# Layer one of a four-layer network: inverses of chunk matrices on packed 32x32 blocks

## What is computed

```python
def rwkv7_step(state, inp):
    r_t, w_t, k_t, v_t, kk_t, a_t = inp
    sa = jnp.einsum('bhvk,bhk->bhv', state, -kk_t)
    state = (state * w_t[:, :, None, :]
             + sa[..., None] * (kk_t * a_t)[:, :, None, :]
             + v_t[..., None] * k_t[:, :, None, :])
    y = jnp.einsum('bhvk,bhk->bhv', state, r_t)
    return state, y
```

## Time and profile before

| | us |
|---|---|
| median of three timed runs (1768.96 to 1769.55) | 1769.27 |
| the profiled execution | 1763.46 |
| its span, first to last instruction | 1761.7 |
| TensorE busy, share of the span | 1678.9, 95% |
| VectorE busy | 1279.4, 73% |
| ScalarE busy | 804.2, 46% |
| GpSimd busy | 827.7, 47% |
| TensorE weight loads, beside the products | 1287.2, 73% |

### The profile page before, as it was taken

How to read it: one execution, slowest core, us unless ns; L and a number is a source line. 1 busy time by engine, 2 the same in 40 slices (tenths; PEclk the granted TensorE clock), 3 DMA queues, 4 the chain that set the end, 5 groups by cost and what they waited for, 6 DMA issues and landing times.

```text
span 1761.7 us, 34351 instructions
## 1 busy us (share of the span) xinstructions
PE 1678.9 (95%) x13932; PEld 1287.2 (73%) x13932; DVE 1279.4 (73%) x2255; ACT 804.2 (46%) x1489; POOL 827.7 (47%) x727
## 2 busy tenths in 40 slices
PE   5899999999999899989999999999999999999997
PEld 5677777787787667757777777787777778777766
DVE  7599999999999788268998777535887536355553
ACT  3534444444453173365534444434767533444443
POOL 3544354354353245457883222544555545545433
PEclk9999999999999999999999999999999999999998
DMA  7212312312313133212221111133222232433322
GB/s 305 93 65 64 119 52 71 121 50 74 121 51 132 37 91 129 86 60 72 84 85 59 37 37 37 49 96 108 77 80 74 87 102 76 139 121 112 114 57 90
DMA packets 51885, 154.84 MB, mean 88 GB/s; under 512 B 5888, under 2 KB 12032, under 8 KB 51600
## 3 DMA queue, kind: packets, MB, share of 16 engines
q1 hardware_dynamic: 51728, 152.65, 26.7%
HBM read 150.50 MB, written 2.13 MB: 87 GB/s over the span
## 4 chain that ended last, share of the span: by engine, by line
PE 37%; DVE 13%; issue 3%; ACT 3%; POOL 2%; DVEq 0%; POOLq 0%; ACTq 0%
PE bank L524 8%; PE bank L528 8%; PE bank L525 8%; PE bank L2350 3%; DVE best L2458 2%; DVE lru_xc L2842 2%; DVE score L2461 2%; PE bank L3067 1%; PE bank L2380 1%; DVE probs_t L2505 1%; PE bank L3082 1%; POOL w_lo L498 1%; PE bank L570 1%; DVE score L2445 1%; PE bank L571 1%
## 5 line engine op out<-in xcount | busy, mean ns | idle before, releaser
L498 POOL TENSOR_TENSOR w_lo<-raw,w_hi 128x512 fp32r<-128x512 f32 (+2 forms) x434 | 581.3, 1355 | 587.7 <-ACT w_hi L480 573.6
L524 PE MATMUL bank<-h_hi,w_hi 128*128 128x512 f32 x1368 | 573.6, 419 | 10.2 <-ACT h_hi L977 2.2
L528 PE MATMUL bank<-h_lo,w_hi 128*128 128x512 f32 x1368 | 539.2, 394 | 7.6 <-DVE h_lo L945 5.7
L525 PE MATMUL bank<-h_hi,w_lo 128*128 128x512 f32 x1368 | 537.5, 393 | 0.0
L480 ACT ACTIVATE w_hi<-raw 128x512 fp32r<-128x512 f32 (+2 forms) x434 | 247.6, 603 | 247.4 <-PE bank L528 162.1
L524 PEld LDWEIGHTS bank<-h_hi,w_hi 128*128 128x128 f32 x1368 | 258.7, 189 | 99.2 <-issue 39.1
L528 PEld LDWEIGHTS bank<-h_lo,w_hi 128*128 128x128 f32 x1368 | 258.2, 189 | 72.6 <-DVE h_lo L945 10.8
L525 PEld LDWEIGHTS bank<-h_hi,w_lo 128*128 128x128 f32 x1368 | 259.3, 190 | 57.0 <-issue 9.3
L1581 DVE SCALAR_TENSOR_TENSOR ya<-padded,vecs,ya 128x512 f32<-128x512 f32 x240 | 217.4, 906 | 3.9
L3143 DVE CUSTOM_DVE_ANT_0 fox_probs<-bank,fox_keybias 128x128 f32<-128x128 f32 (+3 forms) x64 | 28.9, 489 | 84.6 <-PE bank L3067 84.3
L524 PE MATMUL bank<-own_hi,w_hi 128*128 128x512 f32 x208 | 83.2, 400 | 3.9 <-POOL w_lo L498 3.9
(11 more groups left out here) (410 smaller groups left out, 2865.6 us busy)
## 6 DMA issues: line engine op xcount, KB each, us to landing
raw<-even_in SPq DMA_DIRECT2D x57, 512.0 KB, 3.6
raw<-odd_in SPq DMA_DIRECT2D x39, 512.0 KB, 3.5
raw<-ada SPq DMA_DIRECT2D x32, 512.0 KB, 4.2
raw<-fox_in SPq DMA_DIRECT2D x25, 512.0 KB, 3.5
raw<-lru_in SPq DMA_DIRECT2D x24, 512.0 KB, 3.5
ada_first<-ada SPq DMA_DIRECT2D x16, 512.0 KB, 13.4
raw<-even_out SPq DMA_DIRECT2D x16, 512.0 KB, 3.5
raw<-odd_out SPq DMA_DIRECT2D x16, 512.0 KB, 3.5
```

The source lines that it names most:

```text
L498: e.tensor_tensor(k.w_lo[s % NSPLIT][:, at], k.raw[n % NRAW][:, at], k.w_hi[s % NSPLIT][:, at].bitcast(F32), ALU.subtract).then_inc(*did(" ...
L524: e.matmul(out, hi[:, w], x[i][0], start=start and i == 0, stop=False, skip_group_check=True)
L525: e.matmul(out, lo[:, w], x[i][0], start=False, stop=False, skip_group_check=True)
L528: m = e.matmul(out, hi[:, w], x[i][1], start=False, stop=stop and i == kt - 1, skip_group_check=True)
```

## The change

The inverse is made on 32x32 blocks that are packed side by side. With 32 columns for each of eight matrices and four partition quarters, a buffer [128, 256] holds the 32 diagonal blocks of the 16 matrices, and half of a W buffer is enough. `N` is computed so that the diagonal blocks of both kinds of quarter come to lie in the same columns (48 narrower products for 16), and ScalarE also copies the whole. Helper `quarters` replaces `four`: 32 products of 32x32 on the four diagonal tiles, into 256 columns of one bank. The transposed squares are still second sets of products on TensorE (`sq1_t`, `sq2_t`), copied by VectorE; N transposed, and both turns of the merges, are transposes of VectorE. The first merge stays inside the packed blocks. The last merge gives the one off-diagonal 32x32 block of each matrix, and copies put the packed inverses into PT (ScalarE the upper halves, VectorE the rest). MM holds three blocks of 64 columns a chunk, not four. The start masks change with this.

Apart from that, `out_scalar` and `out_gpsimd` get `begun`, set for even, odd and fox: the weights of the third out block are rounded ahead of the activations. In fox the early roundings, their rests and the first two out blocks get other places in the order.

```diff
@@ -1008,6 +1004,8 @@
 
     def blocks():
         yield 0.0
+        if begun:
+            round_ahead(k, e, need, did, k.nth[(name, *out_order()[0])] + NSPLIT)
...
 
-    def four(name, p, lhsT, rhs, until, *ready):
-        (bank,), free = banks(name, p, 1, until)
+    def quarters(name, p, lhsT, rhs, until, *ready):
+        bank, free = k.work.take(*until)
+        k.bank[name, p, 0] = bank
         wait(*free, *ready)
         for n in range(2 * TT):
-            h, c = divmod(n, TT)
-            for g, gs in HALVES:
-                m = mul(bank[gs, at_chunk(n)], lhsT[gs, h, c, :], rhs[gs, h, c, :])
+            cols = slice(n * KB, (n + 1) * KB)
+            for qs in QUARTERS:
+                m = mul(bank[qs, cols], lhsT[qs, cols], rhs[qs, cols])
         m.then_inc(*did("multiplied", name, p))
 
...
+                            j, col = 2 * c + g, (c % 2) * 3 * CH + x * 2 * CH
+                            m = mul(bank[h][gs, col:col + (2 - x) * CH].rearrange("p (a t) -> p a t", t=CH), src[hs, j, :],
+                                    AR[hs, x:, j, :])
             m.then_inc(*did("multiplied", ("mm", half), p))
         yield at["N"]
...
+        taken = [k.work.take(("activated", "N", p, h)) for h in range(2)]
...
         for c in range(TT):
             for g, gs in HALVES:
                 for h, hs in HEADS:
...
+                    j = 2 * c + g
+                    out, right = taken[h][0][:, at_chunk(c)], B[hs, j, :]
+                    mul(out[QUARTERS[2 * g], 0:KB], AR[hs, 0, j, 0:KB], right[:, KB:])
+                    mul(out[QUARTERS[2 * g], KB:], AR[hs, 0, j, 0:KB], right[:, 0:KB])
+                    m = mul(out[QUARTERS[2 * g + 1], :], AR[hs, 0, j, KB:], right)
...
         yield at["sq1"]
...
+        quarters("sq1", p, N_t, N, [("activated", "sq1", p)], ("made", "N_t", p))
+        quarters("sq1_t", p, N, N_t, [("made", "sq1", p)])
         yield at["sq2"]
...
+        quarters("sq2", p, N2_t, N2, [("activated", "sq2", p)], ("activated", "sq1", p), ("made", "sq1", p))
+        quarters("sq2_t", p, N2, N2_t, [("made", "sq2", p)])
         yield at["sq2p"]
...
+        quarters("sq2p", p, N2, inner, [("made", "sq2p", p)], ("pooled", "inner", p))
         yield at["sq3"]
...
+        quarters("sq3", p, N4_t, N4, [("activated", "sq3", p)], ("activated", "sq2", p), ("made", "sq2", p))
         yield at["sq3p"]
...
+        quarters("sq3p", p, N4, inner, [("made", "sq3p", p)], ("made", "sq2p", p))
         yield at["sq4"]
...
+        quarters("sq4p", p, N8, inner, [("made", "sq4p", p)], ("activated", "sq3", p), ("made", "sq3p", p))
+        yield at["off0"]
+        quarters("off0", p, below, inner, [("activated", "off0", p)], ("pooled", "below", p), ("made", "sq4p", p))
+        yield at["merge0"]
+        quarters("merge0", p, N_t, N, [("made", "merge0", p)], ("made", "turn0", p), ("activated", "off0", p))
+        yield at["off1"]
+        bank, free = k.work.take(("activated", "off1", p, 0), ("activated", "off1", p, 1))
+        k.bank["off1", p, 0] = bank
+        wait(*free, ("made", "merge0", p), ("activated", "N", p, 1))
+        for n in range(2 * TT):
+            h, c = divmod(n, TT)
+            for g in range(2):
+                m = mul(bank[QUARTERS[2 * g], n * KB:(n + 1) * KB], k.NN[QUARTERS[2 * g + 1], h, c, 0:KB],
+                        inner[QUARTERS[2 * g + 1], n * KB:(n + 1) * KB])
+        m.then_inc(*did("multiplied", "off1", p))
+        yield at["merge1"]
+        bank, free = k.work.take(("made", "merge1", p))
+        k.bank["merge1", p, 0] = bank
+        wait(*free, ("made", "turn1", p), ("activated", "off1", p, 0), ("activated", "off1", p, 1))
+        for n in range(2 * TT):
+            cols = slice(n * KB, (n + 1) * KB)
+            for q, qs in enumerate(QUARTERS):
...
+def solve_buffers(k):
+
+    N, N_t, N2, N2_t, N4, N4_t, N8, below = (w[:, s, :, :].rearrange("p c t -> p (c t)") for w in k.W for s in range(2))
...
+            ready(("multiplied", "N", p), ("pooled", "masks"))
+            e.tensor_tensor(squares_of(N)[:, h * TT:(h + 1) * TT, :], chunks(got("N", p, h)[:, 0:TT * CH])[:, :, KB:],
+                            k.within16[:, :].unsqueeze(1).to_broadcast([P, TT, KB]), ALU.mult).then_inc(*did("made", "N", p, h))
+
+        def turn(dst, src, label, *steps):
+            yield at[label]
+            ready(*steps)
+            e.transpose(dst, src).then_inc(*did("made", label, p))
+
+        def copy(dst, label):
+            yield at[label]
+            ready(("multiplied", label + "_t", p))
+            e.tensor_copy(dst, got(label + "_t", p)[:, 0:2 * TT * KB]).then_inc(*did("made", label, p))
+
+        def add(label, *steps):
+            yield at[label[:3] if label == "sq4p" else label]
+            ready(("multiplied", label, p), *steps)
+            e.tensor_tensor(inner, got(label, p)[:, 0:2 * TT * KB], inner, ALU.add).then_inc(*did("made", label, p))
+
+        yield from turn(N_t, N, "N_t", ("made", "N", p, 0), ("made", "N", p, 1))
+        yield from copy(N2_t, "sq1")
+        yield from copy(N4_t, "sq2")
+        yield from add("sq2p", ("pooled", "inner", p))
+        yield from add("sq3p", ("made", "sq2p", p))
+        yield from add("sq4p", ("made", "sq3p", p))
+        yield from turn(N_t, inner, "turn0", ("made", "sq4p", p))
+        yield from add("merge0", ("made", "sq4p", p))
+        yield from turn(N2_t, inner, "turn1", ("made", "merge0", p))
+        yield at["merge1"]
+        ready(("multiplied", "merge1", p))
+        e.tensor_copy(PT[:, :, :, KB:].rearrange("p h c t -> p (h c) t"), squares_of(got("merge1", p)[:, 0:2 * TT * KB])).then_inc(
+            *did("made", "merge1", p))
 
...
+        for h in range(2):
+            ready(("made", "N", p, h), ("pooled", "below", p - 1) if p else None)
+            e.activation(k.NN[:, h, :, :], chunks(got("N", p, h)[:, 0:TT * CH]), ACT.Copy).then_inc(*did("activated", "N", p, h))
         yield at["sq1"]
...
+        copy(N2, "sq1")
...
+        copy(N8, "sq3")
+        yield at["off0"]
+        copy(N, "off0")
+        yield at["off1"]
+        for g in range(2):
+            qs = QUARTERS[2 * g]
+            ready(("multiplied", "off1", p))
+            e.activation(N2[qs, :], got("off1", p)[qs, 0:2 * TT * KB], ACT.Copy).then_inc(*did("activated", "off1", p, g))
+        ready(("made", "merge0", p))
+        e.activation(k.PT[:, :, :, 0:KB].rearrange("p h c t -> p (h c) t"), squares_of(inner), ACT.Copy, scale=k.upper[:, :]).then_inc(
+            *did("activated", "upper", p))
         yield at["U0"]
...
+        ready(("made", "N_t", p))
+        e.tensor_tensor(squares_of(inner), squares_of(N_t), every_square(k.ident32), ALU.add).then_inc(*did("pooled", "inner", p))
+        yield at["below"]
+        ready(("activated", "N", p, 0), ("activated", "N", p, 1))
+        e.tensor_tensor(squares_of(below), k.NN[:, :, :, KB:].rearrange("p h c t -> p (h c) t"), every_square(k.below16),
+                        ALU.mult).then_inc(*did("pooled", "below", p))
 
     def split(name, key, at):
...
-    return fox_end("fox_g", DT - 1) + 0.1 + 0.3 * i
+    return fox_end("fox_g", DT - 1) + 0.1 + 0.05 * i
 
 
...
         for cb in range(2):
-            at = FOX_TILES + 0.2 + 3 * cb
+            at = FOX_TILES - 0.5 + 0.9 * cb
             yield from out_block(k, e, need, did, "fox", "fox_out", k.fox_out[0], cb, 0,
-                                 [at + (i + 0.5) / 4 for i in range(DT // 2)])
+                                 [at + 0.1 * i for i in range(DT // 2)])
 
     merge(chain(projections(2, None), out_blocks()),
           in_tiles(FOX_TILES, (0, front), (FOX_LAG + 1, at_pair_end(finish)), (FOX_LAG, back)))
...
+                yield fox_y_time(i) + 0.5
                 own_low(e, need, did, "fox", i, k.fox_out[0], fox_y_source(k), [])
 
```

More of the change, by code:

```diff
@@ L27 @@
 IH = 8
-MERGES = (16, 32)
 TOPK = min(256, T // 4)
@@ L46 @@
 HEADS = HALVES
+QUARTERS = [slice(q * KB, (q + 1) * KB) for q in range(P // KB)]
 SIGNALS = {"tensor": ("projected", "multiplied"), "vector": ("made", "modulated", "tapped"),
@@ L1000, in out_tensor, with out_scalar @@
     square_tensor(k, e, need, did, nxt, both, sq)
-def out_scalar(k, e, need, did, s, name, pairs, src, src_ready, sq, nxt, stage, last=(), beside=(), gain=None, early=0, free=None):
+def out_scalar(k, e, need, did, s, name, pairs, src, src_ready, sq, nxt, stage, last=(), beside=(), gain=None, early=0, free=None, begun=False):
     n = len(pairs)
@@ L1071, in out_vector, with out_gpsimd @@
     merge(*last, *beside, blocks())
-def out_gpsimd(k, e, need, did, s, name, pairs, src, src_ready, stage, last=(), early=0, free=None):
+def out_gpsimd(k, e, need, did, s, name, pairs, src, src_ready, stage, last=(), early=0, free=None, begun=False):
     n = len(pairs)
@@ L1123 @@
         tA mm0 bonus_sum' tV k0 w_up gate0' k1 k2 k3 gate1' gate2' gate3' f_sum2 k4 k5 gate4' mm1 N gate5' gate6' k6
```

(23 more changed lines are left out.)

203 lines of the change are left out of this document (63 added, 140 removed).

## The result

The changed kernel takes 1791.53 us (median of four runs, 1786.2 to 1795.91) against 1769.12 us for the kernel before beside it (1767.58 to 1769.55): ratio 1.0132, 95% interval 1.0117 to 1.0147. It is 22 us slower, where 32 us less was forecast. The profiled execution took 1786.20 us, its span is 1784.5 us.

The account below looks back on a forecast made before the run. TensorE's own work was taken to bound the kernel, VectorE second. Seven pairs at 3.5 us, 3.2 for the last pair and 4.3 at the stage ends gave 32 us less: 1769.3 to 1737 us, range 1725 to 1760.

Parts of the forecast that it names:

- A packed step at 0.56 us: Layer one's inverse on TensorE: 32 products of 32x32, 64 matmuls in 16 rounds of 35 ns, against 0.955 us a squaring.
- Rivals 1 and 2: Packed-step rounds cost 48 ns, 1756 us in all, chance 0.17; or stay at 60 ns, 1772 us, chance 0.08.
- rival 4: Row tiles writing one bank take turns: 2.2 us a packed step, 1880 us in all; chance 0.03.
- rounding down for TensorE's fuller instruction stream, 3.5 us: TensorE's net gain in layer one, 3.6 us a pair, rounded to 3.5 to allow for more instructions.
- Rival 3: TensorE's instruction stream limits at 20 ns an instruction: 4.7 us a pair slower, 1803 us in all; chance 0.08.
- four starts in 0.03 us: Four instructions starting inside a burst's first 0.03 us, cited against the instruction stream being the limit.
- The prediction's own sign of error: Wrong if a packed step exceeds 0.7 us, or is right while TensorE's stage waits exceed 2 us a pair through VectorE's order.
- The wait of sq3 for VectorE, 0.6 us a pair: In layer one's inverse, TensorE's sq3 waits for VectorE's copy of the transposed square; 0.6 us a pair charged.
- 58.3 forecast: VectorE's work in layer one falls 3.9 us, from 62.2 to 58.3 us a pair, beside a 63.1 us period.
- The ends: Ends of three stages: weights rounded before activations save 1.0 + 1.8 us of w_lo waits, plus 1.5 in the last layer.
- 0 and 4 as ends: Range in us for the last layer's stage-end gain, taken as 1.5 us.
- twice the wait and none of the last layer's 1.5 us: Slow end of the forecast's own spread: sq3's 0.6 us wait doubled, no last-layer gain; put at 1746 us.

## Why the prediction was wrong

**What bounds the kernel** held: TensorE before and after, VectorE second.

**A packed step at 0.56 us** nearly held, as long as instructions are at hand: 0.62 us a step, 39 ns a round (0.62 / 16) against 35. Rivals 1 and 2 (48 and 60 ns) fall. So does rival 4: 64 matmuls on four row tiles of one bank took 0.62 us, not 2.2. The Trainium skill, TensorEngine Tiling (Array Packing), Gotcha 1, says that row tiles can't be in one bank at a time; here the trace doesn't agree. Of the floor of about 25 ns that the Trainium skill states (TensorE: Matmul & The Clock Gate, under "Wait — 56ns, not 53.3ns?") the prediction left open whether it counts per pass: a round of 39 ns is below twice 25, so it doesn't.

**The step that failed** is "rounding down for TensorE's fuller instruction stream, 3.5 us", 0.1 us a pair for a cost that came to 4.2 us of pauses: the price of a step was read from bursts of 8 to 64 matmuls and used for ten steps nearly in a row. Within what has been read ahead it is right. Beyond it the chip brought 256 instructions in 3.45 to 3.73 us, 13.5 to 14.6 ns each, 27 to 29 ns a matmul. Rival 3 had this mechanism with a chance of 0.08. It counted matmuls without their weight loads, so its limit of 20 ns a matmul was even too mild, and it took the limit for a uniform rate where it is a supply with a small store. Its evidence against, four starts in 0.03 us, came from inside that store and couldn't speak on the supply. The packets were there to be read on the page of before (111 of 16 KB in the instruction queue). By ten steps x 128 instructions x 14 ns = 18 us, for steps budgeted at 5.6, less what is read ahead and what the work between them lets come in, a loss was in reach. The prediction's own sign of error, waits above 2 us a pair with the step right, came true, but by the stream and not by VectorE's order.

**A second term wasn't in the sum at all**: the granted clock. The pauses that the stream makes are long enough to bring it down, in every pair. The groups of TensorE by line, 142 to 580 us, show a part of the cost in the wide matmuls (count, busy us, mean ns):

```profile
L524 PE MATMUL bank<-h_hi,w_hi 128*128 128x512 f32 x294 | 133.8, 455 | 0.0
L525 PE MATMUL bank<-h_hi,w_lo 128*128 128x512 f32 x294 | 118.2, 402 | 0.0
L528 PE MATMUL bank<-h_lo,w_hi 128*128 128x512 f32 x294 | 117.8, 401 | 0.0
```

Before, the means were 439, 392 and 392: 294 x (16 + 10 + 9) ns = 10 us over 438 / 69.7 = 6.3 pairs, 1.6 us a pair. So the pair nearly adds up: 69.7 measured, less 4.2 of pauses at issue (26.5 / 6.3), less 1.6, is 63.9. Forecast was 63.1, or 62.5 without the wait for VectorE that didn't come. Ten packed steps of 0.62 us instead of 0.56 are 0.6 of the 1.4 us between; the rest is open. That the two terms are nearly the whole loss is worked out so, not shown by a kernel without them.

**The wait of sq3 for VectorE, 0.6 us a pair**, doesn't show in the changed kernel; the pauses at issue stand in its place. **VectorE** came out as worked out or better: 425 ns for an add of 256 columns, 438 for a transpose, 545 for mm; busy 355.46 of 438 us, 56.6 us a pair, against 58.3 forecast.

**The ends** were put at 4.3 us and gave 2 (0.5 to 3.5). The w_lo waits went as said. Mis-sized are layer one, where the shift of the activations' rounding was to stay covered and 0.7 us came back, and the last layer, where 1.5 us were taken and of 4.4 us of waits (3.33 and 1.05) 3.6 came back for the activations' halves; its "0 and 4 as ends" holds that.

**A sum of the prediction** is off and without effect: with twice the wait and none of the last layer's 1.5 us its terms give 7 x 2.9 + 3.2 + 2.8 = 26.3 us less, 1743 us and not 1746.

## What to carry over

Count instructions, not only array time: a stretch of TensorE in which short products follow each other took no less than about 14 ns an instruction here beyond what had been read ahead, so smaller but more numerous products can lose there. Price such a stretch from the packets of the instruction queue. If a transposed operand can be had with one instruction of an engine that has room (here 437 ns on VectorE), that beats 128 short instructions on TensorE. And a pause on TensorE can cost more than its length, as the clock may fall behind it: it did at 3.7 us in every pair, but at 1.4 to 2.9 us only some of the time, so read the granted clock around each pause.

## What the runs showed of the hardware

- Instructions reach TensorE in packets of 16 KB, 256 instructions; in a close run one every 3.45 to 3.73 us, though the transfer engines were at 2 to 3%.
- f32 matmuls of 32x32 by 32 columns on four row tiles that write one bank start 9.7 ns apart while read-ahead instructions last (1.24 us for 128), so their weight loads fit beside them.
- One idle stretch of 3.7 us a pair in work of an otherwise full TensorE brought the granted clock from 1.00 to 0.50 every time; in the changed kernel it stayed there for 4 to 10 us. A pause of 1.46 us did it too, one of 2.37 and one of 2.86 us didn't. All packed steps of a pair but the last, with only a 0.69 us pause, ran at 1.00.
